# Value projections of the first layer: chunks of 512 rows by 512 columns, products of 512 columns, in two banks

## The chip, the cores and the metric

The kernel runs on one core of a Trainium2 chip. The metric is the device time of one execution in microseconds; the number to go by is the median over several runs. One more execution was taken under the hardware profiler, and every row of this document comes from it.

## The reference, cut to what matters

Two small transformer-like networks run one after the other on a sequence of 256 tokens with 1024 features. The change touches only the first layer's input projection, and of it only the value parts `va` and `vb` of the two attention branches, each 256 tokens by 512 features:

```python
h = modulate(rms_norm(x, g_mix[l]), sh_m, sc_m)
proj = jnp.einsum('bsd,de->bse', h, w_in[l])          # 256 x 1024 times 1024 x 5120
qa, ka, va, qb, kb, vb, gate_logits = jnp.split(proj, splits, axis=-1)
oa = moba_attention(to_heads(qa, N_HEADS_MOBA), to_heads(ka, N_HEADS_MOBA), to_heads(va, N_HEADS_MOBA), rel_bias)
ob = stick_breaking_attention(to_heads(qb, N_HEADS_SB), to_heads(kb, N_HEADS_SB), to_heads(vb, N_HEADS_SB))
```

Queries and keys are wanted with features on the partitions, values with tokens on the partitions.

## The kernel before, in words

All weights of both networks come from memory as one stream of chunks of 1 MB, each 128 partitions by 2048 float32 values. SyncE (queue SP) issues the loads in a fixed order (`ORDER`) into a ring of four buffers `raw`; a load waits until VectorE is done with the chunk four places earlier. There are two kinds of chunks: "lin" chunks, which TensorE multiplies, and "mod" chunks, which VectorE alone reduces to shifts and scales (L848). In the part of the program this document is about, lin chunks and mod chunks alternate.

A float32 product is made of three products of a shorter type, fp32r. For each lin chunk ScalarE makes the high part `w_hi` by a cast (L382, called `split` in its program), VectorE the low part `w_lo` by a subtraction (L881, also `split`), each into a ring of three slots, and TensorE runs `triple`: high by high, and the two cross products (L1416). The activations have the same two parts, `h_hi` and `h_lo`.

The first twelve lin chunks, numbered j = 0 to 11, are the queries, keys and values of the two branches: within each group of six, j % 6 = 0, 1 are queries, 2, 3 keys, 4, 5 values. Before the change every one of them is 1024 rows by 256 columns. Query and key chunks go through `features` (weights stationary, 256 tokens moving, eight row tiles, two halves of 128 features). Value chunks go through `tokens` (L1438 to L1444): 128 tokens of the activation are stationary and 256 columns of the weights move; two token halves by eight row tiles by three products are 48 products of 256 columns. Every chunk's result fills one PSUM bank, `bank[j % 2]`, so banks 0 and 1 alternate. ScalarE copies the bank to `proj[:, j]` (L460), which raises the semaphore `proj_evac`.

The order around this is written out by hand, one program for each engine. TensorE, ahead of chunk j, waits for `lo_done` (VectorE's low part) and for `proj_evac` to reach j - 1, that is for the copy of chunk j - 2, whose bank it takes. ScalarE's loop over j first makes the high part of chunk j + 2, for which it waits until that chunk has arrived from memory, and then waits for TensorE and copies chunk j:

```python
for j in range(LIN_GATE):
    if j:
        split(j + 2)
    ...
    act.wait_ge(sem("lin_done"), LIN_OPEN + j + 1)
    nc.scalar.activation(proj[:, j, :], bank[j % 2][:, :], ACT.Copy, ...).then_inc(sem("proj_evac"), 1)
```

The high part of chunk j + 2 also waits until TensorE is done with chunk j - 1, whose slot it takes. After chunk 11 TensorE waits for all twelve copies and goes on with the attention scores (L1541), between which the gate chunks (j = 12 to 19) stand.

Of the kernel before, what the change touches and what calls it, by code (L numbers as in the profile page):

```python
# [10 lines left out]
ACT = mybir.ActivationFunctionType  # L11
AX_X = mybir.AxisListType.X

P = 128
T = 256
D = 1024
KT = D // P
# [5 lines left out]
SPL = 3  # L23
# [3 lines left out]
QK = 0.125  # L27
# [16 lines left out]
LIN_OPEN = 1  # L44
# [80 lines left out]
def build(nc, xs_d, cond_d, vec_d, rel_d, w_d, fw_d, c0_d, c1_d, c2_d, c3_d, diff_d, out_d):  # L125
    ctx = ExitStack()
    with ctx:
# [5 lines left out]
        def sem(name):  # L133
            if name not in sems:
                sems[name] = ctx.enter_context(nc.semaphore(name))
            return sems[name]
# [23 lines left out]
        bank = [psum[:, i, :] for i in range(4)]  # L160
# [3 lines left out]
        proj = arena[:, 0:6144].rearrange("p (c n) -> p c n", n=512)  # L164
# [90 lines left out]
        def halves(b):  # L255
            return b[:, 0:T], b[:, T:2 * T]
# [111 lines left out]
        def _(act):  # L368
# [82 lines left out]
# [3 lines that stand above are left out]
                if j == 7:  # L454
                    act.wait_ge(sem("c0_loaded"), 16)
                    act.wait_ge(sem("c1_loaded"), 16)
                    nc.scalar.copy(ident16, c0[:, C0["ident"]:C0["ident"] + P]).then_inc(sem("mask16_set"), 1)
                    nc.scalar.copy(past16, past).then_inc(sem("mask16_set"), 1)
                act.wait_ge(sem("lin_done"), LIN_OPEN + j + 1)
                nc.scalar.activation(proj[:, j, :], bank[j % 2][:, :], ACT.Copy,  # L460
                                     scale=QK if j % 6 < 2 else 1.0).then_inc(sem("proj_evac"), 1)
                if j == 2:
                    act.wait_ge(sem("bias_row"), 1)
                    nc.scalar.copy(urow, bank[3][0:8, 0:384]).then_inc(sem("bias_row_out"), 1)
                    act.wait_ge(sem("bias_row_out"), 1)
                    act.dma_start(diff_d, urow).then_inc(sem("bias_stored"), 16)
                if j == 4:
                    act.wait_ge(sem("bias_stored"), 16)
                    for h in range(TREV):
                        load_trev(h)  # L470
# [42 lines left out]
            for h in range(NH):  # L513
                j, p = LIN_GATE + h, h // 2
# [100 lines left out]
            for k in range(KT):  # L615
                nc.scalar.activation(gain_rows[:, k, :], c0[:, C0["ones"]:C0["ones"] + P], ACT.Copy,
                                     scale=gain_col[:, k:k + 1]).then_inc(sem("gain_rows"), 1)
# [83 lines left out]
            for t in range(5):  # L701
                if t < 4:
                    act.wait_ge(sem("ln_scaled"), t + 1)
                    me.mark(nc.scalar.activation(conv[:, t, :], conv[:, t, :], ACT.Silu, bias=col("ln_b", t),
                                                 scale=col("ln_g", t)))
# [38 lines left out]
            for i in range(3):  # L744
                j = LIN_OIN + i
# [68 lines left out]
            for k in range(KT):  # L814
# [3 lines left out]
                                     scale=col("final_norm", k)).then_inc(sem("last_scaled"), 1)  # L818
# [590 lines left out]
        def _(pe):  # L1409
# [3 lines left out]
            def triple(out, w, x, start, stop, skip=False):  # L1413

                for n, (a, b) in enumerate(((0, 0), (0, 1), (1, 0))):
                    last = mm(out, w[a], x[b], start=start and n == 0, stop=stop and n == 2, skip_group_check=skip)  # L1416
                return last

            def whl(slot, a, n):
                return w_hi[:, slot, a:a + n], w_lo[:, slot, a:a + n]  # L1420

            def hhl(k, a, n):
                return h_hi[:, k, a:a + n], h_lo[:, k, a:a + n]
# [11 lines left out]
                        last = triple(outs[m], whl(slot, 256 * k + P * m, P), hhl(hk, a, n), i == 0, i == KT - 1)  # L1435
                last.then_inc(sem("lin_done"), 1)

            def tokens(j, slot, outs, a):  # L1438

                pe.wait_ge(sem("lo_done"), j + 1)  # L1440
                for m in range(2):
                    for k in range(KT):
                        last = triple(outs[m], hhl(k, a + P * m, P), whl(slot, 256 * k, 256), k == 0, k == KT - 1)
                last.then_inc(sem("lin_done"), 1)  # L1444

            def sum_squares(name, ks=range(KT)):
# [67 lines left out]
            first_chunks(0, (6, 7))  # L1514
            first_chunks(1, (6, 7))
            for j in range(2, LIN_GATE):
                if j >= 2:
                    pe.wait_ge(sem("proj_evac"), j - 1)
                if j % 6 < 4:
                    features(j, j % SPL, halves(bank[j % 2]), 0, T)  # L1520
                else:
                    tokens(j, j % SPL, halves(bank[j % 2]), 0)

            def q_of(h, branch, a, b):
                t, p0 = h // 2, HD * (h % 2)
# [73 lines left out]
            for h in range(NH):  # L1599
                j, p = LIN_GATE + h, h // 2  # L1600
# [17 lines left out]
            for i in range(4):  # L1618
                j = LIN_BR + i
# [4 lines left out]
                for m in range(4):  # L1624
# [3 lines left out]
                    for k in range(4):  # L1628
                        last = triple(out, whl(j % SPL, 512 * k + P * m, P), hhl(4 * (i % 2) + k, T, T), k == 0, k == 3)
                last.then_inc(sem("lin_done"), 1)  # L1630
            pe.wait_ge(sem("gate_evac"), 8)
            for half in range(2):
                pe.wait_ge(sem("mixed_lo"), half + 1)
                for i in range(2):
                    j = LIN_OUT + i
                    if not half:
                        pe.wait_ge(sem("lo_done"), j + 1)
                    for m in range(2):
                        for k in range(4 * half, 4 * half + 4):
                            last = triple(halves(bank[i])[m], whl(j % SPL, 256 * k + P * m, P), hhl(k, 0, T),  # L1640
                                          m == 0 and k == 0, k == KT - 1, skip=True)
                    if half:
                        last.then_inc(sem("lin_done"), 1)
            for i in (2, 3):
                j = LIN_OUT + i
# [6 lines left out]
                for m in range(2):  # L1652
                    if m:
                        pe.wait_ge(sem("out_evac"), 6)
                    for k in range(KT):
                        last = triple(bank[1 - m][:, 0:T], whl(j % SPL, 256 * k + P * m, P), hhl(k, 0, T), k == 0, k == KT - 1)
# [38 lines left out]
            j = LIN_EIN - 1  # L1695
# [13 lines left out]
            for k in range(KT):  # L1709
                last = mm(bank[2][:, 0:T], ones, gain_sq[:, k, :], start=(k == 0), stop=(k == KT - 1))  # L1710
# [303 lines left out]
def k8(w):  # L2014

    n = w.shape[1] // 256
    return list(w.reshape(8, P, n, 256).transpose(2, 1, 0, 3).reshape(n, P, CHUNK))
# [8 lines left out]
def k4(w):  # L2026
    n = w.shape[1] // 512
    return list(w.reshape(4, P, n, 512).transpose(2, 1, 0, 3).reshape(n, P, CHUNK))
# [93 lines left out]
```

## Time and profile before

| | us |
|---|---|
| median of 3 runs (lowest, highest) | 784.41 (784.31, 784.53) |
| the profiled execution, its own time | 784.45 |
| its span in the profile | 782.6 |
| TensorE busy | 763.1 (97%) |
| VectorE busy | 652.0 (83%) |
| ScalarE busy | 386.3 (49%) |

The span starts with the first instruction that the profiler sees; 1.85 us of the execution lie around it. Times in the rows are microseconds from the span's start. "PE" is TensorE, "PEld" its loading of the stationary operand, "DVE" VectorE, "ACT" ScalarE, "SP" the queue of SyncE. A row of the timeline gives the start, the duration, the engine, the line and the operation; in brackets stands how long the engine had been idle, and what ended that. Matmuls overlap in the pipeline, so the time that one adds to a row of them is read from the distance of their starts and not from their duration.

### The profile page before, as it was taken

The page shows a single profiled execution, that of the slowest core. Times are in us where ns is not written, and L with a number is a line of the kernel's source. Part 1 is how long each engine was busy: PE and PEld are TensorE (multiplying, and loading weights), DVE is VectorE, ACT ScalarE, POOL GpSimd, SP SyncE. Part 2 cuts the span into 40 slices and gives each one's busy share as a digit, 9 for nine tenths or more (in the row PEclk, how much of TensorE's full clock was granted, in tenths as well). Part 3 has the DMA queues.
Part 4 walks back from the last instruction along what each step waited for, and adds up shares of the span by engine and source line. Part 5 has one row for each costly group of instructions (what it writes and reads, how often), then busy time and mean ns, then how long its engine had stood idle before and what let it go on. Part 6 is the DMA issues. An engine that isn't in the chain of part 4 may idle for free.

```text
span 782.6 us, 13194 instructions
## 1 busy us (share of the span) xinstructions
PE 763.1 (97%) x5504; PEld 698.1 (89%) x5504; DVE 652.0 (83%) x1009; ACT 386.3 (49%) x522; POOL 46.4 (6%) x32
## 2 busy tenths in 40 slices
PE   8899999999999999999999999999999999999996
PEld 3599999999999999999999998888777899999995
DVE  5987878995896899999798679999989966986753
ACT  4543555558447545445446532322464345355752
POOL 0000000000000322232122000000000000000000
PEclk9799999999999999999999999999999999999999
DMA  9899998666673567666654341213106542563101
GB/s 357 350 401 381 376 369 292 252 218 207 215 267 111 165 258 272 240 252 262 220 207 171 108 162 54 108 55 108 54 1 238 215 158 106 227 225 143 61 2 54
DMA packets 25928, 154.96 MB, mean 198 GB/s; under 512 B 2660, under 2 KB 7309, under 8 KB 7821
## 3 DMA queue, kind: packets, MB, share of 16 engines
q1 hardware_dynamic: 22940, 150.37, 52.0%
q10 hardware_dynamic: 2930, 3.76, 1.5%
q8 instruction: 43, 0.70, 0.4%
q14 instruction: 15, 0.12, 0.0%
HBM read 153.06 MB, written 1.06 MB: 197 GB/s over the span
## 4 chain that ended last, share of the span: by engine, by line
PE 84%; DVE 9%; ACT 3%; issue 2%; DMA 1%; POOL 1%; SPq 1%; DVEq 0%; ACTq 0%
PE psum L1416 71%; DVE w_lo L848 3%; DVE w_lo L881 2%; DMA raw<-in_w 1%; PE psum L1451 1%; PE psum L1742 1%; PE psum L1917 1%; PE psum L1893 1%; PE psum L1905 1%; PE psum L1728 1%; PE psum L1592 1%; ACT w_hi L382 1%; DVE arena L1085 1%; DVE arena L1090 0%; PE psum L1707 0%
## 5 line engine op out<-in xcount | busy, mean ns | idle before, releaser
L1416 PE MATMUL psum<-h_hi,w_hi 128*128 128x256 f32 (+1 forms) x1312 | 395.8, 302 | 4.0 <-DVE h_lo L953 2.7
L1416 PE MATMUL psum<-h_lo,w_hi 128*128 128x256 f32 (+1 forms) x1312 | 391.6, 298 | 0.0
L1416 PE MATMUL psum<-h_hi,w_lo 128*128 128x256 f32 (+1 forms) x1312 | 391.5, 298 | 0.0
L1416 PEld LDWEIGHTS psum<-h_hi,w_hi 128*128 128x128 f32 x1312 | 250.8, 191 | 15.0 <-DVE h_lo L953 3.1
L1416 PEld LDWEIGHTS psum<-h_lo,w_hi 128*128 128x128 f32 x1312 | 250.9, 191 | 7.8 <-issue 0.2
L1416 PEld LDWEIGHTS psum<-h_hi,w_lo 128*128 128x128 f32 x1312 | 250.8, 191 | 7.5
L881 DVE TENSOR_TENSOR w_lo<-raw,w_hi 128x2048 fp32r<-128x2048 f32 x93 | 212.7, 2287 | 34.6 <-ACT w_hi L382 33.7
L382 ACT CAST w_hi<-raw 128x2048 fp32r<-128x2048 f32 x93 | 177.1, 1907 | 46.4 <-DMA raw<-in_w 42.0
L848 DVE SCALAR_TENSOR_TENSOR w_lo<-raw,cond 128x1024 fp32r<-128x1024 f32 x88 | 119.5, 1395 | 8.3 <-PE psum L1416 7.5
L848 DVE SCALAR_TENSOR_TENSOR w_lo<-raw,arena 128x1024 fp32r<-128x1024 f32 x48 | 56.7, 1219 | 8.9 <-ACT arena L425 7.0
L352 POOL TENSOR_TENSOR arena<-arena 128x512 f32<-128x512 f32 x11 | 26.1, 2369 | 365.5 <-ACT arena L603 365.5
L1416 PE MATMUL psum<-g_hi,w_hi 128*128 128x256 f32 x160 | 45.7, 286 | 1.7 <-POOL g_lo L355 0.9
L1141 DVE SCALAR_TENSOR_TENSOR arena<-att,vec,arena 128x256 f32<-128x256 f32 x116 | 47.0, 477 | 0.1
L1416 PE MATMUL psum<-g_lo,w_hi 128*128 128x256 f32 x160 | 45.3, 283 | 0.0
L1416 PE MATMUL psum<-g_hi,w_lo 128*128 128x256 f32 x160 | 45.3, 283 | 0.0
L575 ACT ACTIVATE arena<-psum,vec 128x256 f32<-128x256 f32 x44 | 22.4, 561 | 37.5 <-PE psum L1416 34.4
L399 ACT ACTIVATE att<-xs 128x256 f32<-128x256 f32 x32 | 12.4, 412 | 44.4 <-DVE xs L1248 24.1
L1416 PEld LDWEIGHTS psum<-g_hi,w_hi 128*128 128x128 f32 x160 | 30.7, 192 | 2.1 <-issue 1.1
L1416 PEld LDWEIGHTS psum<-g_lo,w_hi 128*128 128x128 f32 x160 | 30.7, 192 | 0.0
L1416 PEld LDWEIGHTS psum<-g_hi,w_lo 128*128 128x128 f32 x160 | 30.7, 192 | 0.0
L416 ACT ACTIVATE h_hi<-att,modv 128x256 fp32r<-128x256 f32 x48 | 22.6, 505 | 12.2 <-DVE att L915 8.3
L1416 PE MATMUL psum<-w_lo,h_hi 128*128 128x256 f32 (+1 forms) x96 | 26.9, 280 | 0.0
(227 smaller groups left out, 795.1 us busy)
## 6 DMA issues: line engine op xcount, KB each, us to landing
raw<-in_w SPq DMA_DIRECT2D x141, 1024.0 KB, 5.0
xs<-in_xs SPq DMA_DIRECT2D x1, 1024.0 KB, 10.1
consts<-diff ACTq DMA_DIRECT2D x8, 128.0 KB, 8.0
xs<-in_xs ACTq DMA_DIRECT2D x1, 1024.0 KB, 10.2
out<-xs SPq DMA_DIRECT2D x2, 384.0 KB, 2.8
consts<-in_c ACTq DMA_DIRECT2D x1, 512.0 KB, 3.5
arena<-in_c ACTq DMA_DIRECT2D x1, 448.0 KB, 3.2
consts<-in_c ACTq DMA_DIRECT2D x1, 256.0 KB, 7.1
```

The lines of the kernel that those rows point to most:

```text
L352: nc.gpsimd.tensor_tensor(cv, cv, cg, ALU.mult).then_inc(sem("ffn_mult"), 1)
L382: nc.scalar.copy(w_hi[:, slot, :], raw[:, rslot, :]).then_inc(sem("hi_done"), 1)
L399: nc.scalar.activation(square_tmp(name)[:, k, :], xs[:, k, s * T:(s + 1) * T], ACT.Square).then_inc(sem(f"sq_{name}"), 1)
L416: nc.scalar.activation(h_hi[:, k, s * T:(s + 1) * T], norm_tmp[:, k, :], ACT.Identity, bias=shift_col(sh, k, v), scale=1.0).then_inc(sem(" ...
L575: nc.scalar.activation(dst[:, t, :], (src or bank[which])[:, t * T:(t + 1) * T], ACT.Identity, bias=col("b_conv", tile), scale=col("w_conv ...
L848: last = nc.vector.scalar_tensor_tensor(w_lo[:, slot, D * t:D * (t + 1)], raw[:, rslot, D * t:D * (t + 1)], 1.0, c, ALU.mult, ALU.mult, ac ...
L881: nc.vector.tensor_tensor(w_lo[:, slot, :], raw[:, rslot, :], w_hi[:, slot, :].bitcast(F32), ALU.subtract).then_inc(sem("lo_done"), 1)
L1085: me.mark(nc.vector.scalar_tensor_tensor(dst[:, t, 1:T], src[:, t * T:(t + 1) * T - 1], col("w_conv", 44 + tile), dst[:, t, 1:T], ALU.mult ...
L1141: nc.vector.scalar_tensor_tensor(out, src, weight, acc, ALU.mult, ALU.add).then_inc(sem("conv_tap"), 1)
L1416: last = mm(out, w[a], x[b], start=start and n == 0, stop=stop and n == 2, skip_group_check=skip)
L1451: last = mm(bank[2 + s][:, s * T:(s + 1) * T], ones, square_tmp(name)[:, k, :], start=(k == 0), stop=(k == KT - 1))
L1592: last = mm(values[HD * b:HD * (b + 1), out], v_of(2 * p + b, branch, m), w[:, b, part], start=m == 0, stop=m == 1)
```

## The change

For the values (j % 6 = 4 and 5) a chunk is now 512 rows by 512 columns: chunk 4 holds the upper 512 rows of all 512 value columns, chunk 5 the lower 512 rows. A sum over 1024 rows is half made by chunk 4 and half by chunk 5. Bank 0 takes tokens 0 to 127 and bank 1 tokens 128 to 255, with all 512 columns each, and both stay open over both chunks. A product now moves 512 columns: two token halves by four row tiles by three products are 24 for each chunk. ScalarE copies nothing after chunk 4 and two banks after chunk 5, in the loop's step j = 5 and behind the high part that this step makes. The bytes loaded, their order and the number of chunks stay the same.

```diff
-                act.wait_ge(sem("lin_done"), LIN_OPEN + j + 1)
-                nc.scalar.activation(proj[:, j, :], bank[j % 2][:, :], ACT.Copy,
-                                     scale=QK if j % 6 < 2 else 1.0).then_inc(sem("proj_evac"), 1)
+                for m in range(2 if j % 6 == 5 else 0):
+                    if m:
+                        act.wait_ge(sem("lin_done"), LIN_OPEN + j + 1)
+                    else:
+                        act.wait_ge(sem("values_half"), j // 6 + 1)
+                    nc.scalar.copy(proj[:, j - 1:j + 1, T * m:T * (m + 1)], bank[m].rearrange("p (c n) -> p c n", c=2)
+                                   ).then_inc(sem("proj_evac"), 1)
+                if j % 6 < 4:
+                    act.wait_ge(sem("lin_done"), LIN_OPEN + j + 1)
+                    nc.scalar.activation(proj[:, j, :], bank[j % 2][:, :], ACT.Copy,
+                                         scale=QK if j % 6 < 2 else 1.0).then_inc(sem("proj_evac"), 1)
...
-            def tokens(j, slot, outs, a):
+            def value_rows(j):
+
+                half = j % 2
                 pe.wait_ge(sem("lo_done"), j + 1)
                 for m in range(2):
-                    for k in range(KT):
-                        last = triple(outs[m], hhl(k, a + P * m, P), whl(slot, 256 * k, 256), k == 0, k == KT - 1)
+                    if half == 0:
+                        pe.wait_ge(sem("proj_evac"), j - 1 + m)
+                    for k in range(4):
+                        last = triple(bank[m], hhl(4 * half + k, P * m, P), whl(j % SPL, 512 * k, 512),
+                                      half == 0 and k == 0, half == 1 and k == 3)
+                    if half and m == 0:
+                        last.then_inc(sem("values_half"), 1)
                 last.then_inc(sem("lin_done"), 1)
...
             for j in range(2, LIN_GATE):
-                if j >= 2:
+                if j % 6 < 4:
                     pe.wait_ge(sem("proj_evac"), j - 1)
-                if j % 6 < 4:
                     features(j, j % SPL, halves(bank[j % 2]), 0, T)
                 else:
-                    tokens(j, j % SPL, halves(bank[j % 2]), 0)
+                    value_rows(j)
...
-            lin += k8(part[b + n])
+            lin += k8(part[b + n]) if n < 2 else k4(part[b + n][:512]) + k4(part[b + n][512:])
```

How the instructions stand on ScalarE before, from the high part of chunk 5 on (L382 makes a high part, L460 copies a bank, L429 loads the attention bias):

```order
L382 CAST w_hi<-raw 128x2048 [waits lin_done,arrived0]
L460 ACTIVATE arena<-psum 128x512 [waits lin_done]
L382 CAST w_hi<-raw 128x2048 [waits lin_done,arrived2]
L460 ACTIVATE arena<-psum 128x512 [waits lin_done]
L429 DMA consts<-diff 128x256 [waits bias_stored]
L429 DMA consts<-diff 128x256 x2
L382 CAST w_hi<-raw 128x2048 [waits lin_done,arrived0]
L460 ACTIVATE arena<-psum 128x512 [waits lin_done]
L382 CAST w_hi<-raw 128x2048 [waits lin_done,arrived2]
L460 ACTIVATE arena<-psum 128x512 [waits lin_done]
```

In this order they are the high part of 5, the copy of 3, the high part of 6, the copy of 4, the bias loads, the high part of 7, the copy of 5, the high part of 8 and the copy of 6. The same piece of ScalarE's program with the change (L468 copies a query or key bank, L464 a value bank):

```order
L382 CAST w_hi<-raw 128x2048 [waits lin_done,arrived0]
L468 ACTIVATE arena<-psum 128x512 [waits lin_done]
L382 CAST w_hi<-raw 128x2048 [waits lin_done,arrived2]
L429 DMA consts<-diff 128x256 [waits bias_stored]
L429 DMA consts<-diff 128x256 x2
L382 CAST w_hi<-raw 128x2048 [waits lin_done,arrived0]
L464 COPY arena<-psum 128x2x256 [waits values_half]
L464 COPY arena<-psum 128x2x256 [waits lin_done]
L382 CAST w_hi<-raw 128x2048 [waits lin_done,arrived2]
L468 ACTIVATE arena<-psum 128x512 [waits lin_done]
```

The copy between the high parts of 6 and 7 is gone, and two copies stand behind the high part of 7. On TensorE chunk 4 now begins with these rows, has a second wait ahead of its second half of the tokens, and is followed by chunk 5 and then by chunk 6, whose first rows are the last three:

```order
L1424 MATMUL psum<-w_hi,h_hi 128x512 [waits proj_evac,lo_done]
L1424 MATMUL psum<-w_lo,h_hi 128x512
L1424 MATMUL psum<-w_hi,h_lo 128x512
...
L1424 MATMUL psum<-w_hi,h_hi 128x512 [waits proj_evac]
...
L1424 MATMUL psum<-h_hi,w_hi 128x256 [waits lo_done,proj_evac]
L1424 MATMUL psum<-h_lo,w_hi 128x256
L1424 MATMUL psum<-h_hi,w_lo 128x256
```

The wait of chunk 6 asks for the fifth copy, as before; the fifth copy was that of chunk 4 and is now that of bank 0 after half of chunk 5.

## Rows read from the trace of the kernel before

**Rows 1.** The page: the busy time of all engines, and its slices

```profile
PE 763.1 (97%) x5504; PEld 698.1 (89%) x5504; DVE 652.0 (83%) x1009; ACT 386.3 (49%) x522; POOL 46.4 (6%) x32
```

**Rows 2.** The chain that ended last, in order of time: start, duration, what

```profile
41.23 60.75 PE psum L1416 x504
101.98 0.02 issue
102.00 0.61 ACT arena L460
102.61 0.04 issue
102.65 0.93 PE psum L1541 x8
...
183.74 36.18 PE psum L1416 x300
...
233.66 23.41 PE psum L1416 x192
257.31 0.57 ACT arena L575
```

**Rows 3.** The timeline of TensorE: starts of chunks 4 and 6, end of chunk 11

```profile
55.73 0.28 PE L1416 MATMUL psum<-w_hi,h_hi 128*128 128x256 f32 x1
...
67.25 0.28 PE L1416 MATMUL psum<-h_hi,w_hi 128*128 128x256 f32 x1
...
101.69 0.28 PE L1416 MATMUL psum<-w_hi,h_lo 128*128 128x256 f32 x1
```

**Rows 4.** The timeline of TensorE, products of 512 columns in the second network

```profile
479.74 0.39 PE L1416 MATMUL psum<-h_hi,w_hi 128*128 128x512 f32 x1
...
480.87 0.39 PE L1416 MATMUL psum<-h_hi,w_lo 128*128 128x512 f32 x1
```

**Rows 5.** The timeline of ScalarE around chunks 5 to 7, and later

```profile
55.31 1.91 ACT L382 CAST w_hi<-raw 128x2048 fp32r<-128x2048 f32 x1 [2.37 <-DMA raw<-in_w]
57.13 0.58 ACT L460 ACTIVATE arena<-psum 128x512 f32<-128x512 f32 x1
61.94 1.91 ACT L382 CAST w_hi<-raw 128x2048 fp32r<-128x2048 f32 x1 [4.22 <-DMA raw<-in_w]
...
63.75 0.58 ACT L460 ACTIVATE arena<-psum 128x512 f32<-128x512 f32 x1
67.41 1.91 ACT L382 CAST w_hi<-raw 128x2048 fp32r<-128x2048 f32 x1 [3.08 <-DMA raw<-in_w]
69.22 0.59 ACT L460 ACTIVATE arena<-psum 128x512 f32<-128x512 f32 x1
```

**Rows 6.** Weight loads by line, 40 to 105 us: issue to landing, who waited

```profile
  ACT w_hi L382: 28.4, 9
DMA to landing us min/median/max: 6.4/6.9/8.3
```

**Rows 7.** Windows, 67 to 76 us (columns: busy by engine, PEclk, DMA share, GB/s)

```profile
67.00:76.00 9.00, 9.00 (x77) 9.00 (x76) 6.95 (x10) 4.80 (x4) 0.00 (x0) 1.00 1.03 415
```

**Rows 8.** ScalarE's copies with a two-piece output, L511

```profile
L511 ACT CAST h_hi<-psum x3: 585/585/585, 130.6 to 168.8; 128x512 fp32r<-128x512 f32 x3
```

**Rows 9.** Windows with the clock's fall, its rise, and a short standstill

```profile
18.00:19.00 1.00, 1.00 (x3) 0.37 (x2) 1.00 (x3) 0.00 (x0) 0.00 (x0) 0.92 1.02 426
19.00:28.00 9.00, 7.40 (x15) 1.93 (x14) 8.83 (x18) 4.19 (x6) 0.00 (x0) 0.50 0.78 317
29.00:30.00 1.00, 1.00 (x8) 0.79 (x7) 0.93 (x4) 1.00 (x2) 0.00 (x0) 0.96 0.63 262
40.00:41.00 1.00, 0.00 (x0) 0.00 (x0) 0.82 (x3) 0.85 (x2) 0.00 (x0) 1.00 0.96 382
```

**Rows 10.** The timeline of TensorE around that fall, that rise and that standstill

```profile
16.29 4.70 PE L1480 MATMUL psum<-arena 1*128 1x512 f32 x8
23.96 5.71 PE L1498 MATMUL psum<-zeros 128*128 128x512 bf16 x14
41.23 0.38 PE L1416 MATMUL psum<-h_hi,w_hi 128*128 128x256 f32 x1 [1.56 <-DVE h_lo L953]
```

## The prediction

> **What bounds the kernel now.** I read the page first, then the chain of waits, then the timelines of the stretch that is edited. The page has TensorE busy for 763.1 of 782.6 us [rows 1]: a delay or a gain on TensorE counts as long as TensorE is what its neighbours wait for. The chain says so for the edited stretch: from 41.23 us on, 504 products of one line follow each other for 60.75 us without a step of another engine, and behind them stand only one copy by ScalarE and the first attention scores [rows 2]. These 504 are the end of chunks 0 and 1 and all of chunks 2 to 11. So chunks 4, 5, 10 and 11 lie on the path that sets the end, and so does every wait that is put among them.
>
> How close the other engines follow is the second thing to see. ScalarE's high part of chunk 7 starts at 67.41 after 3.08 us of idling that the arrival of the weights ends; TensorE had begun chunk 6 at 67.25 [rows 3, 5]. The loads take a median of 6.9 us from issue to landing and the DMA engines are full, at a share of 1.03 [rows 6, 7]. In nine waits of 28.4 us in total ScalarE waits for them [rows 6]. So the high parts come at the pace of the memory, about one chunk ahead of use, and no faster TensorE makes them come earlier. Whatever is placed behind a high part in ScalarE's program comes at that pace too.
>
> **The change, part by part.**
>
> *Wider products.* Before, 12 × 48 products stand at equal distance: from the start of chunk 4 at 55.73 to that of chunk 6 at 67.25 are 96 of them in 11.52 us, 0.120 each [rows 3]. Products of 512 columns are in the trace, in the second network: 479.74 to 480.87 are five distances, 0.226 each [rows 4]. Two chunks of values become 48 products of 0.226, 10.85 us in place of 11.52. That is 0.67 us for each branch, 1.34 in all, if nothing waits. Columns streamed are the same; what is saved is the constant part, 0.014 us for each of 96 products that are gone. The Trainium skill ("TensorE: Matmul & The Clock Gate", Part 1, "Wait — 56ns, not 53.3ns?") gives this constant part as 2.5 ns on a warm array. By it the saving would be 96 × 2.5 ns, an estimate of 0.24 us, and the sum below 0.55 us higher; the rows here show over five times as much, and I take the rows.
>
> *Fewer loads of the stationary operand* (192 become 96): they run beside the products, and the distances above already hold what they cost. Nothing more.
>
> *Chunk 4's waits.* The first wait is for the copy of chunk 2, long made. The second is new: bank 1 must be free of chunk 3. That copy starts at 57.13 and takes 0.58 [rows 5], so it is over at 57.71. The first half of chunk 4 keeps TensorE until 55.73 + 12 × 0.226 = 58.44. Hidden, with 0.7 us to spare. If this cover were gone, each microsecond would count.
>
> *Chunk 6's wait, the term that decides.* Chunk 6 takes bank 0 and waits for the fifth copy. Before, this was the copy of chunk 4, started at 63.75 and over at 64.33 [rows 5], 2.9 us before chunk 6 began at 67.25. Now bank 0 is in use until the middle of chunk 5 and its copy stands in ScalarE's order behind the high part of chunk 7. ScalarE can't begin that before the weights land, at 67.41. What is queued behind this waiting cast is both value copies, and TensorE waits for the first. The row says where a copy behind this cast starts: 69.22 [rows 5]. From the start of a copy to the first product that waited for it are 0.65 us (102.00 to 102.65, rows 2). So chunk 6 begins at 69.87 in place of 67.25: **2.62 us later**. TensorE would have been free at 55.73 + 10.85 = 66.58, so it stands still for about 3.3 us, and the first branch's saving of 0.67 is lost in that.
>
> *Is the copy itself dearer?* Its output is now two pieces of 256. The nearest row is a copy of the same size with a two-piece output: 0.585 us against 0.58 to 0.59 [rows 5, 8]. Nothing; from below and above ± 0.01.
>
> *Chunk 7* waits for the sixth copy, of bank 1, right behind the fifth: over by 70.5, when chunk 6 has just begun. Hidden. The other copies of chunks 6 to 9 come later with their chunks, each one chunk ahead of its reader.
>
> *Chunks 10 and 11.* Chunks 6 to 9 take 4 × 5.76 from 69.87 on, so chunk 10 starts at 92.9. Its weights and the copies it waits for are there (before, it started at 90.3). It saves 0.67 with chunk 11. The high part of chunk 13 now stands ahead of both copies, and it waits until chunk 10 is done, at about 98.7; it ends at 100.6, before chunk 11's first half of the last products ends at 101. The last copy is behind the last product as before, so the step to the scores costs the same. Hidden, with 0.4 us to spare for the first copy, and for the end it only matters that both copies are not later than the last product, where 3 us are left.
>
> Sum on TensorE at the start of the scores: +2.62 − 0.67 = **+1.95 us**.
>
> *Does it last to the end?* After this the chain runs on TensorE (300 products from 183.74 on, 192 from 233.66 on), and where it leaves TensorE at 257.31 it goes to a ScalarE step that waited for the last of these [rows 2]. A delay goes through one for one. The loads get slack instead, which nobody waits for.
>
> *The clock.* The granted clock of the stretch is 1.00, the 2.4 GHz level [rows 7]. A standstill of 3.3 us is new there, so its cost must be bounded from other rows. From above: at 16.29 TensorE went from dense products to eight products with one row of the array in use, and the clock fell to 0.50, the 1.2 GHz level, within 18 to 19: the mean of 0.92 there puts it at 18.84, 2.6 us later. Dense products began again at 23.96, and the mean of 0.96 in 29 to 30 puts the rise at 29.1: some 5.1 us of dense work at the lower level, of which half is lost, 2.6 us [rows 9, 10]. From below: over the standstill of 1.56 us before 41.23 the clock stayed at 1.00, cost 0 [rows 9, 10]. The new standstill, with no product at all, is longer than both, so a fall is rather likely. For its price I have no better than the middle of the two ends, 1.3 us; how fast the clock comes back after this gap is open. The same page of the Trainium skill (Part 1, "What's actually happening") says that throttled is the default and activity releases it; the fall in rows 9 agrees.
>
> With it: 784.45 (the profiled execution, 0.04 above the median of the runs) + 1.95 + 1.3 = **787.7 us**.
>
> **The rivals.**
>
> *A. Stall without a fall of the clock.* TensorE was dense before and is dense after the gap, unlike at 16 to 24 us, where sparse work went on for longer. Then 784.45 + 1.95 = 786.4 us.
>
> *B. Not slower: the wait is hidden.* Place: the wait of chunk 6 for bank 0. It costs nothing if the high part of chunk 7 and the copy are done by 66.58, that is, if its weights land 3.3 us earlier than now, by 64.1. Then both branches save, 784.45 − 1.34 = 783.1 us. Against it: the load's slot comes free by VectorE's work on chunk 5, which the change doesn't move, and the DMA engines are full [rows 7]. This is also the case in which the change does what it says.
>
> *C. The delay is absorbed later.* Where TensorE waits for VectorE after 257 us, the loads that now run further ahead could let VectorE catch up. It would need VectorE's row of steps to begin before TensorE's last product of 257.31, and the chain says it begins after it [rows 2]. Partly absorbed: about 785.2 us.
>
> **How the numbers follow.** Stall with a fall of the clock 0.5, case A 0.33, B 0.07, C 0.1. About 0.2%, 1.6 us, is what a measurement of this kernel can tell from no change, so slower means above 786.0. The forecast case lies above it, A mostly (0.3 of its 0.33, since the landing at 67.41 can shift by a few tenths), B and C within it, but for 0.02 of B. That gives slower 0.8, same 0.18, faster 0.02. The range reaches from a little under A to the upper bound of the clock's cost, 784.45 + 1.95 + 2.6 = 789.0: from 785.6 to 789.1. It leaves out B and most of C.
>
> **What would show it.** In the timeline of the changed kernel the products of the values should stand 0.226 apart; chunk 6 should begin near 69.9 with an idle time of about 3.3 us released by ScalarE's copy, L464; the two L464 copies should follow directly on the cast that starts near 67.4. The clock by windows after 67 should be at 0.50 for a few microseconds, or not (case A). The scores should begin near 105.9 (case A: 104.6) in place of 102.65, and the distance should be the same at the end. Chunk 6 starting before 67.2, or ScalarE's idle time before the cast of chunk 7 being released by anything but the load, would make the prediction wrong.

## The result, and the profile after

| | before | with the change |
|---|---|---|
| median, us | 784.44 (8 runs) | 787.4 (8 runs) |
| lowest to highest, us | 784.27 to 784.9 | 784.8 to 788.9 |
| the profiled execution, us | 784.45 | 786.03 |
| its span, us | 782.6 | 784.2 |

The ratio of the changed kernel to the one before is 1.003, with a 95% interval of 1.0018 to 1.0043. It is slower by 0.2 to 0.4%, and its runs lie 4.1 us apart where those of before lie 0.6 us apart. The ratios here and below weigh all runs and are not quotients of the medians; only two runs of one version, 794.82 and 794.91 us, are left out of its ratio as slow ones. The profiled execution is one of the better ones, 1.4 us under the median.

The code has 96 products fewer, and the page counts 98 fewer; against [rows 1] TensorE's busy time hardly moves:

```profile
PE 761.0 (97%) x5406; PEld 693.7 (88%) x5408; DVE 652.1 (83%) x1009; ACT 386.8 (49%) x522; POOL 46.4 (6%) x32
```

The chain of waits of the changed kernel from 60 us on (start, duration, what), to be held against [rows 2]:

```profile
60.01 6.85 DMA raw<-in_w
66.89 0.03 ACT w_hi L382
66.91 1.78 issue
68.69 0.59 ACT arena L464
69.28 0.04 issue
69.32 34.21 PE psum L1424 x240
103.56 0.59 ACT arena L464
104.16 0.04 issue
104.20 0.93 PE psum L1554 x8
```

The unbroken row of 504 products is gone. The chain comes from a load of weights over the high part of chunk 7 and the copy of bank 0 to chunk 6, and then on 240 products to the scores, which begin at 104.20 and not at 102.65: 1.55 us later, the 1.6 us by which the span is longer. So the delay does last to the end.

The same on ScalarE's timeline, against [rows 5]:

```profile
61.04 1.92 ACT L382 CAST w_hi<-raw 128x2048 fp32r<-128x2048 f32 x1 [2.96 <-DMA raw<-in_w]
...
66.89 1.90 ACT L382 CAST w_hi<-raw 128x2048 fp32r<-128x2048 f32 x1 [3.93 <-DMA raw<-in_w]
68.69 1.07 ACT L464 COPY arena<-psum 128x512 f32<-128x512 f32 x2
```

And on TensorE's, around the end of chunk 5 and the start of chunk 6, against [rows 3, 4]:

```profile
66.16 0.39 PE L1424 MATMUL psum<-w_lo,h_hi 128*128 128x512 f32 x1
66.39 0.39 PE L1424 MATMUL psum<-w_hi,h_lo 128*128 128x512 f32 x1
69.32 0.39 PE L1424 MATMUL psum<-h_hi,w_hi 128*128 128x256 f32 x1 [2.55 <-ACT arena L464]
```

The wide products stand 0.23 apart, as in the second network. From the start of the last product to the next one are 2.9 us, of which the product itself takes 0.23 and the standstill 2.7, and what releases TensorE is the value copy L464. The two copies took 1.07 us together, so their two-piece output costs nothing. In this execution the clock stayed at its upper level through the gap (columns: busy by engine, clock, DMA share, GB/s):

```profile
68.00:69.00 1.00, 0.00 (x0) 0.00 (x0) 0.11 (x1) 1.00 (x2) 0.00 (x0) 1.00 1.05 437
69.00:70.00 1.00, 0.68 (x5) 0.68 (x6) 1.00 (x1) 0.76 (x2) 0.00 (x0) 1.00 1.03 426
70.00:72.00 2.00, 2.00 (x19) 2.00 (x18) 2.00 (x2) 0.00 (x0) 0.00 (x0) 1.00 0.97 408
```

That profile is the case that I had called A. The question for the experiments is what the median has above it, and whether the stall is all that stands between the change and its gain.

### The profile page after: what moved, and what is told of

It is laid out like the page before. It is cut to its first block, busy times and chain, and to the rows that moved or that the text cites. A ratio compares the mean times of both kernels' runs of the same rounds, so it can differ in the third digit from the quotient of the medians.

```text
span 784.2 us, 12998 instructions
## 1 busy us (share of the span) xinstructions
PE 761.0 (97%) x5406; PEld 693.7 (88%) x5408; DVE 652.1 (83%) x1009; ACT 386.8 (49%) x522; POOL 46.4 (6%) x32
## 4 chain that ended last, share of the span: by engine, by line
PE 80%; DVE 9%; DMA 4%; ACT 3%; issue 2%; POOL 1%; SPq 1%; DVEq 0%; ACTq 0%
PE psum L1424 67%; DMA raw<-in_w 4%; DVE w_lo L856 3%; DVE w_lo L889 2%; PE psum L1465 1%; ACT w_hi L382 1%; PE psum L1755 1%; PE psum L1930 1%; PE psum L1906 1%; PE psum L1918 1%; PE psum L1741 1%; PE psum L1605 1%; DVE arena L1093 1%; DVE arena L1098 0%; PE psum L1720 0%
## 5 line engine op out<-in xcount | busy, mean ns | idle before, releaser
L382 ACT CAST w_hi<-raw 128x2048 fp32r<-128x2048 f32 x93 | 177.1, 1906 | 43.1 <-DMA raw<-in_w 37.6
L923 DVE SCALAR_TENSOR_TENSOR att<-xs,coef,rstd 128x256 f32<-128x256 f32 x32 | 16.6, 545 | 8.9 <-ACT rstd L409 8.8
```

The source lines that it names most:

```text
L382: nc.scalar.copy(w_hi[:, slot, :], raw[:, rslot, :]).then_inc(sem("hi_done"), 1)
L923: nc.vector.scalar_tensor_tensor(norm_tmp[:, k, :], xs[:, k, s * T:(s + 1) * T], coef[:, at + k:at + k + 1], rstd_of, ALU.mult, ALU.mult). ...
```

## Experiments: the stall, the clock and the width

All times are medians; each batch had its own runs of the kernel before on the same chip. With more runs the kernel before shows single high executions too: up to 786.41, 789.22, 786.15 and 788.54 in the four batches. Four kernels ran together first, beside a median of 784.52 for the kernel before (23 runs).

**The wait alone**, in the kernel before:

```diff
                 if j >= 2:
-                    pe.wait_ge(sem("proj_evac"), j - 1)
+                    pe.wait_ge(sem("proj_evac"), j - 1 + (j == 6))
```

> The kernel before, with one wait raised: chunk 6 waits for six copies and not for five, so for the copy of chunk 5 that stands behind the high part of chunk 7. Narrow products and all copies as before. If the stall alone explains the loss: chunk 6 starts 0.65 us behind the start of that copy, 2.1 to 2.7 us late, 786.6 to 787.1 us without a fall of the clock and up to 2.6 more in runs with one, so a median of 787 to 789 and a wide spread again. If the wait is harmless by itself: 784.4.

Measured: 788.17 us (786.51 to 789.01, 6 runs), ratio 1.0038 (1.0026 to 1.005). With nothing but the wait, the kernel before is as slow as with the whole change and as scattered. The median lies in the expected range; chunk 6 starts 2.95 us late and not 2.1 to 2.7, as the high part of chunk 7 could begin only at 67.75 there. Its chain is the changed kernel's, with products of 256 columns:

```profile
67.75 0.02 ACT w_hi L382
67.78 1.78 issue
69.56 0.60 ACT arena L460
70.16 0.04 issue
70.20 36.32 PE psum L1416 x288
```

This execution (789.01) had a fall of the clock right behind the gap:

```profile
69.00:70.00 1.00, 0.00 (x0) 0.00 (x0) 0.25 (x1) 1.00 (x2) 0.00 (x0) 1.00 1.01 343
70.00:72.00 2.00, 1.80 (x8) 1.80 (x9) 2.00 (x2) 0.15 (x1) 0.00 (x0) 0.55 1.00 398
72.00:74.00 2.00, 2.00 (x13) 2.00 (x12) 2.00 (x4) 0.29 (x1) 0.00 (x0) 0.59 1.02 425
```

**The changed kernel once more**, unedited, for its times and another profile.

> The changed kernel once more, for more runs of its times beside the other three and for another profile. Both theories (falls of the clock in some runs, or a landing that varies) expect 784.8 to 788.9 again. If the clock falls in some runs, a profile of such a run shows 0.50 somewhere from 66 to 75 us; with the landing alone chunk 6 starts at another time and the clock stays at 1.00.

Measured: 787.52 us (786.16 to 789.27, 6 runs), ratio 1.0037 (1.0024 to 1.005); the profiled execution took 787.37. Chunk 6 began at 69.18, even a little earlier than in the first profile, yet the 240 products up to the last copy took 1.49 us longer than its 34.21:

```profile
69.18 35.70 PE psum L1424 x240
```

The clock says why:

```profile
69.00:70.00 1.00, 0.82 (x5) 0.82 (x6) 1.00 (x1) 0.62 (x2) 0.00 (x0) 0.74 1.01 417
70.00:72.00 2.00, 2.00 (x11) 2.00 (x11) 2.00 (x2) 0.00 (x0) 0.00 (x0) 0.50 0.99 411
72.00:74.00 2.00, 2.00 (x16) 2.00 (x15) 1.32 (x4) 0.84 (x1) 0.00 (x0) 0.77 1.02 425
```

Eleven products fit into the two microseconds from 70 to 72, where the first profile has nineteen. The means of 0.74 and 0.77 put the fall at about 69.5 and the rise at about 72.9. So one kernel, with 2.8 and 2.9 us between the two starts, has executions with a fall and without, and a fall costs about 1.5 us. With the wait alone there were 3.1 us between the starts, and the clock fell.

**The gap filled** with products on zeros:

```diff
             for j in range(2, LIN_GATE):
+                for _ in range(12 if j == 6 else 0):
+                    mm(bank[3], zeros[:, 0:P], zeros[:, :], start=True, stop=True)
```

> The changed kernel with 12 products on zeros (bf16, 512 columns, into the unused bank 3) between chunks 5 and 6; they take 12 x 0.213 = 2.6 us and lie in the standstill. If falls of the clock make the spread and the median above the profiled run: the clock stays at 1.00, chunk 6 starts as before near 69.3 to 69.9, the median falls to 785.9 to 786.4 and the spread narrows to that of the weights' landing. If the spread comes from the landing alone: median 787.4 and the same spread as the changed kernel.

Measured: 786.51 us (785.57 to 787.41, 11 runs), ratio 1.0021 (1.0013 to 1.003). Chunk 6 starts no earlier, and the clock stays up in this profile (1.00 in every window from 66 to 76 us):

```profile
66.49 2.76 PE L1532 MATMUL psum<-zeros 128*128 128x512 bf16 x12
69.84 0.39 PE L1424 MATMUL psum<-h_hi,w_hi 128*128 128x256 f32 x1 [0.59 <-ACT arena L464]
```

Work of no use at all takes 1.0 us off the changed kernel's median of the same batch and its highest run down from 789.27 to 787.41. That fits falls of the clock in a part of the changed kernel's executions, at 1.5 us for each. The median is 0.1 above what I expected, and a spread of 1.8 us remains. Chunk 6 started between 69.18 and 70.20 in the four stalled profiles, so the landing alone can make some 1.0 us of it.

**The copy first.** ScalarE copies bank 0 ahead of the high part of chunk 7:

```diff
-                if j:
+                if j and j != 5:
                     split(j + 2)
...
                                    ).then_inc(sem("proj_evac"), 1)
+                    if j == 5 and m == 0:
+                        split(7)
```

> The changed kernel, but in step 5 ScalarE copies bank 0 ahead of the high part of chunk 7 (bank 1 behind it). If chunk 6's wait for that copy is the whole loss: chunk 6 starts right behind chunk 5 near 66.6, no idle time of TensorE from 41 to 101, and only the saving of wider products is left: 2 x 0.67, 784.45 - 1.34 = 783.1 us, with a spread of the runs like that of the kernel before (some 0.6 us). If the loss came from something else (the strided copies, the banks held open, the layout of the weights), it stays at 786 to 788.

Measured: 785.36 us (783.25 to 785.91, 11 runs), ratio 1.0005 (0.9996 to 1.0013). The stall is gone: in the profile of an execution of 783.65 chunk 6 starts 0.22 us behind the last product of chunk 5. Its chain:

```profile
41.36 42.83 PE psum L1426 x312
84.21 16.90 PE psum L1426 x96
101.14 0.59 ACT arena L464
```

The stretch takes 59.8 us up to the last copy where it took 60.77 before [rows 2]; 0.3 us are lost in a wait near 84 us. But nine of eleven runs are at 784.7 and above. The expectation came near for the best two, and the median was missed by 2.3 us: something else takes the gain away.

## Experiments: where the gain went once the stall was gone

The second batch ran beside 784.7 us for the kernel before (35 runs).

**The copy first, once more**, for another profile.

> The version with the early copy once more, for another profile and more times. Its profile had no stall at chunk 6 and 0.3 us of waiting at chunk 9; its other runs were 1 to 2.3 us above that profiled one. If late weights are the cause: waits of TensorE or its loading of the stationary operand for VectorE's low parts, 1 to 2 us in total from 60 to 100 us, behind casts that a load ended, with the clock at 1.00. If the clock is: 0.50 somewhere from 40 us on and no such waits.

Measured: 785.12 us (784.59 to 790.53, 12 runs), ratio 1.0012 (1.0 to 1.0024). Neither expectation was it. The clock stayed up, and TensorE waited for no low part. It waited at chunk 10, in the waits from 41.5 to 101 us (engine, what, for whom: us in total, times, longest):

```profile
PE psum L1426 <- ACT arena L470: 1.2, 1, 1.2
```

```profile
91.58 1.91 ACT L382 CAST w_hi<-raw 128x2048 fp32r<-128x2048 f32 x1 [4.33 <-DMA raw<-in_w]
93.39 0.58 ACT L470 ACTIVATE arena<-psum 128x512 f32<-128x512 f32 x1
```

It is the same pattern in the second branch: the second half of chunk 10 wants bank 1, whose copy (chunk 9) stands behind the high part of chunk 11, whose weights landed at 91.58, 2 us later than in the profile of before. In the changed kernel the stall at chunk 6 leaves room for this, since chunk 10 comes 2 us later.

**The same with narrow products**: banks, chunks and waits of the version with the early copy, each product of 512 columns made as two of 256.

```diff
-                        last = triple(bank[m], hhl(4 * half + k, P * m, P), whl(j % SPL, 512 * k, 512),
-                                      half == 0 and k == 0, half == 1 and k == 3)
+                        for c in range(2):
+                            last = triple(halves(bank[m])[c], hhl(4 * half + k, P * m, P), whl(j % SPL, 512 * k + T * c, T),
+                                          half == 0 and k == 0 and c == 0, half == 1 and k == 3, skip=True)
```

> The kernel with the early copy, but every product of 512 columns is made as two of 256, so the chunks, banks, copies and waits are the new ones and only the width is the old one. Product width alone is worth 1.34 us on TensorE: the values' products stand 0.120 apart again and the end of chunk 11 comes 1.3 us later than with wide products, near 102. If TensorE sets the time of this stretch: 784.4 us. If the landing of the weights sets it since the early copy (its median was 785.4 with a best run of 783.3): the median stays at 785 to 785.5, within 0.4 of the wide version.

Measured: 784.57 us (784.25 to 785.95, 11 runs), ratio 0.9999 (0.999 to 1.0007). On TensorE the width does what the sum said:

```profile
41.40 61.06 PE psum L1426 x504
102.48 0.59 ACT arena L464
```

61.06 us against 42.83 + 16.90 = 59.73 with wide products in the first profile of the early copy, each with some 0.3 us of waits in it: 1.33 us for both branches, where I had 1.34. Yet the kernel's median is no better with wide products (785.12 on the same chip), it is 0.55 us worse. The profiles of these two runs don't say why: in the wide one, of 785.16 us, the wait at chunk 10 had already taken the gain, and the scores began at 103.17, in the narrow one, of 784.93 us, at 103.12. In the first profile of the early copy, without that wait, they began at 101.78, and the execution took 783.65. So what is lost in these profiles is lost ahead of the scores; whether more is lost behind them in the runs that have no profile isn't shown yet.

**The weights earlier**: one mod chunk is loaded behind lin chunk 12 and not between 5 and 6, in the version with the early copy and in the kernel before.

```diff
-        n = int(j >= 2) if j < LIN_GATE else 0 if j == LIN_GATE else 2 ...
+        n = int(j >= 2 and j != 5) if j < LIN_GATE else 1 if j == LIN_GATE else 2 ...
```

> The early copy, and the mod chunk that was loaded between lin chunks 5 and 6 is loaded behind lin chunk 12 instead. The weights of chunks 6 to 12 then land up to 2.7 us earlier. If late weights were all that kept the early copy from its 1.34 us: 783.1 us, no wait of TensorE from 41 to 101, a spread under 1 us. If not: 785.4 as before. A loss by the moved chunk itself would show on VectorE behind chunk 12.

> The kernel before with the same mod chunk moved. It was not waiting for weights in its profile, so 784.4, and its rare runs at 785 to 786.4 should be gone if they were late weights. If the moved chunk costs by itself, it shows here: above 784.6. If moving it gains by itself (over 0.3 us), the gain of the version with both edits is not the wide products' alone.

Measured: with the early copy 784.21 us (783.09 to 794.04, 12 runs), ratio 1.0004 (0.9977 to 1.0031); in the kernel before 784.47 us (784.17 to 786.44, 11 runs), ratio 0.9998 (0.9989 to 1.0007). The move neither costs nor gives anything to the kernel before, and its rare runs above 785 (785.02 and 786.44) didn't go away, as they should have if late weights had made them. With the early copy the median is 0.9 us lower than without, and nine of twelve runs are at 784.4 or below, but two took 791.78 and 794.04, and the latter was profiled. TensorE waited once, near 120 us:

```profile
127.47 0.80 PE L1561 MATMUL psum<-consts 128*128 128x128 f32 x2 [7.58 <-DMA consts<-diff]
```

That is not a load of weights. It is the attention bias of heads 3 and 4, which ScalarE's queue loads when the first scores are done (L429). It took 23.2 to 23.4 us to land.

**Other banks.** The third batch ran beside 784.5 us for the kernel before (29 runs). The values' sums go to banks 2 and 3, which nobody uses there once a row of the bias is out of bank 3 (the added wait), and ScalarE's order stays the changed kernel's:

```diff
                     if half == 0:
-                        pe.wait_ge(sem("proj_evac"), j - 1 + m)
+                        pe.wait_ge(sem("proj_evac"), 3 if j == 4 else 6)
+                        if m:
+                            pe.wait_ge(sem("bias_row_out"), 1)
...
-                        last = triple(bank[m], ...
+                        last = triple(bank[2 + m], ...
...
-                    pe.wait_ge(sem("proj_evac"), j - 1)
+                    pe.wait_ge(sem("proj_evac"), j - 3 if j in (6, 7) else j - 1)
```

> The changed kernel with the values' sums in banks 2 and 3, which are free there, in place of 0 and 1; ScalarE's order stays that of the changed kernel. Chunks 6 and 7 then wait for the copies of chunks 2 and 3 and chunks 4 and 10 for none that is late. If the waits for banks were the loss of the change (2.6 us at chunk 6) and of the early copy's runs (the wait of chunk 10's second half for the copy of chunk 9, 1.2 us in the second profile), no wait of TensorE for ScalarE's copies is left from 41 to 101, and the median is 783.2 to 783.8. If late weights held the early copy back, waits for VectorE's low parts stay and the median is 785.

> Banks 0 and 1 as in the changed kernel, the early copy in step 5, and in step 9 the copy of chunk 9 ahead of the high part of chunk 11. The two waits for banks are then met early, as with other banks: 783.3 to 784.0. If the wait at chunk 10 was only one accident of a profile and not why the early copy's median was 785.1 to 785.4, it stays there.

> The version with banks 2 and 3 and the mod chunk between lin chunks 5 and 6 loaded behind lin chunk 12. If late weights still take something from the other banks' version, this gives it back: 783.1 and 0.2 to 0.6 us under that version. If not, the two are the same within 0.2. Rare runs of 790 and more came with the moved chunk and once without it; if the move makes them, they show here and not in the version without it.

Measured: other banks 785.27 us (782.98 to 789.68, 12 runs), ratio 1.0007 (0.9992 to 1.0021); two copies first 785.65 us (782.92 to 794.91, 12 runs), ratio 1.0015 (0.9996 to 1.0035); other banks with the moved chunk 784.43 us (782.92 to 788.95, 12 runs), ratio 0.9999 (0.9987 to 1.0011). All three have executions below everything that the kernel before ever showed (784.05), and none has a median that is better by more than 0.1 us. The expected medians were missed by 1.3 to 1.7 us. In each profile no product of TensorE waits for a copy between 42 and 101 us, so the waits for banks are met. Something is still lost ahead of the scores: with the other banks TensorE waited 0.4 us for low parts, which was the sign named for late weights, and the scores began at 102.49, only 0.16 us earlier than in the kernel before. The high part of chunk 13 stands ahead of both value copies there and began at 99.56, so the scores waited 0.94 us and not 0.69. The other loss is the bias. For the other banks (execution of 785.78):

```profile
PE psum L1561 <- DMA consts<-diff: 1.2, 1, 1.2
```

and for the two copies first (execution of 794.91):

```profile
128.57 0.80 PE L1563 MATMUL psum<-consts 128*128 128x128 f32 x2 [8.24 <-DMA consts<-diff]
```

The loads of this bias, from issue to landing in the window from 100 to 112 us: in the kernel before, with the other banks, and with the two copies first.

```profile
DMA to landing us min/median/max: 7.5/8.3/9.0
```

```profile
DMA to landing us min/median/max: 16.8/16.9/17.0
```

```profile
DMA to landing us min/median/max: 24.0/24.0/24.1
```

In the kernel before this bias is issued at 105.1 and wanted at about 120.1, so some 15 us are covered and 9.0 are needed. What grew is seen one step earlier in the same queue. ScalarE's queue issues the load of the context (1 MB) right behind the last value copy, and the bias 3 us later. Over all profiles, by the time at which the context load is issued:

```
context issued at     context lands after    bias lands after     profiles
100.8 to 101.6        15.1 to 27.2 us        14.9 to 24.1 us      early copy, two copies first, other banks, both with the moved chunk
102.0 to 102.5        10.2 to 14.7 us         7.5 to 13.8 us      before, narrow, early copy again, before with the moved chunk
103.6 to 106.6         9.0 to  9.7 us         6.2 to  6.9 us      changed (twice), gap filled, wait alone
```

From group to group, the earlier the context is issued after 100 us, the longer it takes, and the bias behind it with it; within the first group there is no such order (27.2 us at 101.04, 15.1 at 101.14). A microsecond gained by TensorE before the scores can be given back with interest: the wait at about 120 us was 0 to 8.2 us. The highest runs (790.53, 794.04, 794.91) have a mean clock of only 0.985 to 0.987; in the profiles of the last two the products behind the wait take 0.80 us a pair and not the 0.49 of a run without it, so the long standstill also costs the clock. This is the end of that standstill in the execution of 794.04, with the clock at 0.50 and the DMA engines all but idle:

```profile
126.00:128.00 2.00, 0.53 (x2) 0.53 (x3) 0.00 (x0) 0.00 (x0) 0.00 (x0) 0.50 0.04 14
```

So it isn't the memory as a whole that holds the bias up to the end. Context and bias are 1280 packets of 1 KB. In the execution of 794.04 the 1200th of them starts at 117.45 and the last at 127.10; in the kernel before at 111.37 and 113.72. From 123.5 to 126.7 the packets that are left start 0.35 us apart with a packet of 8 KB of the weights' queue behind each of them, and once those have run out 0.04 us apart. That looks like one of the 16 DMA engines that is behind and serves the two queues in turn, a small packet for a large one; the trace doesn't name the engine.

Where the time was lost can be read from the start of the scores in all profiles:

```
wait for the bias   scores begin at      execution less start of scores     profiles
none                101.78 to 107.19     681.79 to 681.87 us                nine (all but those below)
none                103.17               681.99                             early copy again
1.2 us              102.49               683.29                             other banks
1.4 us              101.79               683.52                             other banks with the moved chunk
7.6 us              101.55               692.49                             early copy with the moved chunk
8.2 us              101.99               692.92                             two copies first
```

Without a wait for the bias nothing changes behind the scores, and an execution is as long as the scores are late. What keeps the versions from their gain is thus two things, late weights ahead of the scores and the late bias behind them, and which of them made a run without a profile slow isn't known.

**The context later.** The context isn't read before 190 us. Its load was moved behind the last bias loads, in the version with the other banks. Beside 784.79 us for the kernel before (17 runs):

```diff
-            act.dma_start(xs[:, :, T:2 * T], xs_d[:, :, T:2 * T]).then_inc(sem("ctx_loaded"), 16)
...
+                if h == 4:
+                    act.dma_start(xs[:, :, T:2 * T], xs_d[:, :, T:2 * T]).then_inc(sem("ctx_loaded"), 16)
```

> The version with banks 2 and 3, and the load of the context (1 MB, on ScalarE's queue, issued right ahead of the attention bias of heads 3 and 4) issued behind the last bias loads instead. In the profiles of three versions without a stall at chunk 6 TensorE waited 1.2 to 8.2 us near 120 us for that bias, which took 17 to 24 us to land. If the bias standing behind the context load and the weights is what keeps the median of these versions 2 us over their best run (782.9): the bias lands in under 14 us, no wait for it near 120, median 783.0 to 783.6, spread under 1 us, no run above 785. If the weights alone crowd out the bias, or something else makes the spread: median 784.5 to 785.5 and a wide spread as before.

Measured: 783.99 us (782.99 to 785.58, 12 runs), ratio 0.9983 (0.9971 to 0.9994). This is the only version that beats the kernel before beyond its interval, by 0.8 us between the medians, and no run is above 785.6, where the kernel before had 787.12 and 788.54 among its 17. The profiled execution is its slowest, and even so shows no wait for the bias, which now lands in 5 us:

```profile
DMA to landing us min/median/max: 4.9/4.9/5.0
```

This one profile can't tell what the move is worth: its bias was issued late, at 106.21, and with an issue at 106.67 it lands in 6.5 us even behind the context (the changed kernel). The DMA engines were also less full from 106 to 112 us, at a share of 0.89 and not 1.03 as with the other banks and the context ahead. What the profile shows instead is late weights. The casts of chunks 7 and 11 began at 68.80 and 92.98, 1.4 and 3.5 us later than before the change, and TensorE waited for low parts. In the waits from 42 to 101 us:

```profile
PE psum L1425 <- DVE w_lo L890: 1.8, 2, 1.1
```

So my expectation was wrong in its numbers: the median is 783.99 and not 783.0 to 783.6, the spread 2.6 us and not under 1, and three runs are above 785. With no wait for the bias the late weights, which I had nearly given up as a cause, are next. What held is that the bias lands in under 14 us and TensorE doesn't wait for it. No run is above 785.6, where five of twelve were above 785.7 with the same banks and the context ahead (on another chip); that speaks for the context's place as a cause of the high runs, and doesn't prove it.

## Why the prediction was right, step by step

*Wider products, 0.67 us for each branch.* Right: 1.33 us for both in the pair of profiles that differ in width alone, 14 ns for each product fewer. The constant part that the Trainium skill ("TensorE: Matmul & The Clock Gate", Part 1, "Wait — 56ns, not 53.3ns?") gives, and by which it would be an estimated 0.24 us, is not what the rows show here. In these products the stationary operand changes with each; whether that makes the difference no run shows.

*Chunk 6's wait, 2.62 us.* Right in mechanism and near in size: 2.07, 1.93 and 2.59 us in the three profiles of the changed kernel and of the one with the gap filled. The weights of chunk 7 landed at 66.89, 66.74 and 67.41, and the last of these is the value I had taken from the one profile of before. That the wait alone does it is shown by the kernel before with one number raised, where chunk 6 came 2.95 us late. The standstill was 2.7 us, from 66.62 to 69.32, and not 3.3, mostly for the same reason.

*Everything hidden.* Chunk 4's second wait, the copies' cost and chunks 7 to 11 were as said. The net at the scores was 1.55 us in the first profile, where I had 1.95. By the sum it would be 2.07 - 0.67 = 1.40; the 0.15 us between are small waits that I can't place.

*One for one to the end.* Right: 1.55 at the scores, 1.6 in the span.

*The clock, 1.3 us.* The fall costs 1.5 us where it happens. What I hadn't said is that both cases occur in one kernel: of its two profiles one has the fall. The median of 787.4 lies between A (786.4) and the forecast (787.7), and is most likely a mixture of both; how many of the runs had a fall isn't known. The middle of two far ends was luck as much as method: the stall came out 0.4 us smaller than forecast and the fall 0.2 us dearer.

*Rivals.* A is the first profile. B, the hidden wait, became real when the wait was taken away, and with it came what the list lacked: a faster TensorE would not have been enough. I had costed case B at 783.1, and that is what the best runs of the versions without the stall give (782.92 to 783.25, with wide products and but for one batch, whose best was 784.59), but their medians are 784.0 to 785.7. The loads behind 101 us were in the trace, with 9 us of landing against 15 us of cover; that looks safe, and I had not asked what an earlier context load would meet.

**Still open:** why the context load takes up to 17 us longer when it is issued one to two microseconds earlier. Its last packets take turns with large ones of the weights, but why some are left so late wasn't tried. That the bias suffers from standing behind the context is likely by the landings and by the runs with the context later, and no pair of profiles with the same weights around it shows it. Also open is what makes the weights of one chunk land up to 2 us later from one execution to the next.

## What to carry to other kernels

A buffer's release is worth what stands ahead of it on the engine that releases it: when two copies are merged into a later step, look up which wait the step begins with. Here it was a load, so TensorE was tied to the memory's pace, and a wait that had 2.9 us to spare became a standstill of 2.7 us. Free buffers elsewhere (banks 2 and 3), or the copy ahead of the cast, take that away. And before a gain is counted, look for the loads that the faster engine triggers earlier: a load that nobody needs soon is better not issued ahead of one that is needed. The only version here that beat the kernel before had that load moved away.

## What the runs showed of the hardware that I had not expected

A gap of 2.8 us between the starts of two products in dense work on TensorE let the clock fall in one execution, and a gap of 2.9 us in another execution of the same kernel did not; the fall cost 1.5 us. Filling the gap with twelve products on zeros took 1.0 us off the median. And two loads of 128 KB took 23 to 24 us to land behind a load of 1 MB on their queue in two executions, and 6.2 to 6.9 us behind the same load in four others; in one of the slow two, only the last 80 of 1280 packets made 10 us of it.
